# Mixture-of-experts stage: split fp32r products in groups of 256 columns replaced by plain fp32 products in groups of 512 columns, read straight from the load rings

## The reference

```python
logits = (xt @ w_router).astype(jnp.float32)
top_v, top_e = lax.top_k(logits, TOP_K)          # 2 of 8 experts
gates = jax.nn.softmax(top_v, -1)
...
def expert_block(args):
    tok, e = args
    xb = x_pad[tok]                              # up to 128 tokens of expert e
    return (jax.nn.silu(xb @ wg[e]) * (xb @ wu[e])) @ wd[e]
...
y = jnp.zeros((n + 1, D_MODEL), jnp.float32).at[buf_tok].add(yb... * buf_gate[:, None])
```

## Time and profile before

| | us |
|---|---|
| median of three runs | 2461.19 |
| the profiled execution, its own time | 2464.63 |
| its span, first to last instruction | 2462.8 |
| TensorE matmul busy / weight load busy | 2159.2 / 1740.0 |
| VectorE / ScalarE / GpSimd busy | 1315.7 / 1067.0 / 143.0 |
| first expert product to last added result | 1607.2 to 2448.4 |

### The profile page before, as it was taken

One profiled execution on the slowest core, in us unless ns is written; L12 is line 12 of the kernel. 1 busy time (PEld: TensorE's weight loads), 2 busy tenths in 40 slices (PEclk: granted clock), 3 DMA queues, 4 the chain that ended last, 5 costly groups with the idle time before them and its releaser, 6 DMA issues. The chain is left out here.

```text
span 2462.8 us, 38086 instructions
## 1 busy us (share of the span) xinstructions
PE 2159.2 (88%) x15542; PEld 1740.0 (71%) x15543; DVE 1315.7 (53%) x1913; ACT 1067.0 (43%) x1688; POOL 143.0 (6%) x176
## 2 busy tenths in 40 slices
PE   6986997799976898888878887699999999999997
PEld 4765996699954675577644454588778787787876
DVE  4125233444313465326733231488888888788885
ACT  3112321333213455224442330267666766667664
POOL 5001140000003100100000000000000000000000
PEclk8997998899988888856889998799999999999998
DMA  5100002554285542203024323489999999999993
GB/s 196 69 1 18 20 21 91 171 165 154 76 254 218 201 158 68 33 1 137 1 111 171 155 110 69 144 288 355 337 319 321 335 329 338 329 324 332 326 338 114
DMA packets 309634, 443.24 MB, mean 180 GB/s; under 512 B 60855, under 2 KB 273031, under 8 KB 306256
## 3 DMA queue, kind: packets, MB, share of 16 engines
q1 hardware_dynamic: 305706, 373.53, 46.1%
q0 software_dynamic: 3456, 67.11, 6.7%
q10 hardware_dynamic: 294, 0.11, 0.0%
HBM read 435.35 MB, written 13.67 MB: 182 GB/s over the span
## 5 line engine op out<-in xcount | busy, mean ns | idle before, releaser
L2763 DVE TENSOR_TENSOR moe.w_gate_up_lo<-mw.w_gate_up,moe.w_gate_up_hi 128x2048 fp32r<-128x2048 f32 x176 | 402.6, 2291 | 121.5 <-ACT moe.w_gate_up_hi L2696 121.3
L2696 ACT CAST moe.w_gate_up_hi<-mw.w_gate_up 128x2048 fp32r<-128x2048 f32 x176 | 335.7, 1909 | 161.5 <-PE moe.b L1050 161.5
L1048 PE MATMUL moe.b<-moe.w_gate_up_hi,moe.x_block_hi 128*128 128x512 f32 x704 | 277.3, 394 | 0.0
L1050 PE MATMUL moe.b<-moe.w_gate_up_hi,moe.x_block_lo 128*128 128x512 f32 x704 | 275.5, 391 | 0.0
L1049 PE MATMUL moe.b<-moe.w_gate_up_lo,moe.x_block_hi 128*128 128x512 f32 x704 | 275.1, 391 | 0.0
L2702 ACT CAST moe.w_down_hi<-mw.w_down 128x1024 fp32r<-128x1024 f32 x176 | 185.2, 1052 | 94.6 <-PE moe.b L1050 79.1
L2763 DVE TENSOR_TENSOR moe.w_down_lo<-mw.w_down,moe.w_down_hi 128x1024 fp32r<-128x1024 f32 x176 | 208.1, 1218 | 18.0 <-ACT moe.w_down_hi L2702 18.0
L1048 PE MATMUL moe.b<-moe.w_down_hi,moe.hidden_t_hi 128*128 128x512 f32 x352 | 148.6, 422 | 21.2 <-issue 18.8
L1050 PEld LDWEIGHTS moe.b<-moe.w_gate_up_hi,moe.x_block_lo 128*128 128x128 f32 x704 | 132.7, 188 | 28.5
L1048 PEld LDWEIGHTS moe.b<-moe.w_gate_up_hi,moe.x_block_hi 128*128 128x128 f32 x704 | 133.1, 189 | 26.3
L1049 PEld LDWEIGHTS moe.b<-moe.w_gate_up_lo,moe.x_block_hi 128*128 128x128 f32 x704 | 133.0, 189 | 26.2
(11 more groups left out here) (615 smaller groups left out, 4187.0 us busy)
## 6 DMA issues: line engine op xcount, KB each, us to landing
mw.w_gate_up<-in_moe_w_gate SPq DMA_DIRECT2D x176, 512.0 KB, 5.9
mw.w_gate_up<-in_moe_w_up SPq DMA_DIRECT2D x176, 512.0 KB, 7.2
mw.w_down<-in_moe_w_down SPq DMA_DIRECT2D x176, 512.0 KB, 6.0
rin.w_rkv<-in_rw_w_rkv SPq DMA_DIRECT2D x3, 4096.0 KB, 18.2
ffn.w<-in_ffn_w_gate SPq DMA_DIRECT2D x11, 1024.0 KB, 5.4
ffn.w<-in_ffn_w_up SPq DMA_DIRECT2D x11, 1024.0 KB, 8.0
ffn.w<-in_ffn_w_down SPq DMA_DIRECT2D x10, 1024.0 KB, 6.0
out_win_kv_sample<-in_state_win_kv SPq DMA_DIRECT2D x1, 8128.0 KB
```

What stands on the lines that cost most here:

```text
L1048: nc.tensor.matmul(out, w_hi, x_hi, start=start, stop=False)
L1050: return nc.tensor.matmul(out, w_lo, x_hi, start=False, stop=stop)
L2696: nc.scalar.copy(gu_hi[:, j % HR], M.wgu[:, j % M.RGU]).then_inc(gu_high, 1)
L2763: return nc.vector.tensor_tensor(out, x, high, ALU.subtract)
```

## The change

In `stage_moe` the split is gone. The normed rows are one fp32 tensor `M.x`, the products are single plain fp32 matmuls whose moving operand is the loaded piece itself, the groups are 512 columns wide (5 of 512 and one of 256 for each expert), gate and up have a bank each, and one buffer each of `H`, `silu`, `hidden_t` and `y` is left. A load piece has two (for the group of 256: four) of the eight row blocks, the rings have 12 pieces of 8 KB and 8 of 4 KB for each partition, and SP refills when TensorE has used a piece. The order on TensorE is `gate_up(T)`, `down(T - 1)`, `turn(T)`. `ahead` fills the larger rings. In `stage_moe_rest` only the gather is changed alike. The diff, cut to its core:

```diff
@@ stage_route, ahead and the block after it
-                for out, src in gate_up_half(M, io, j):
+                for out, src in gate_up_piece(M, io, j):
...
-                    nc.scalar.copy(M.xh[0:m, t, 512 * (n % 2):512 * (n % 2) + 512], bank[2 + n][0:m, :]).then_inc(ev, 1)
+                    nc.scalar.copy(M.x[0:m, t, 512 * (n % 2):512 * (n % 2) + 512], bank[2 + n][0:m, :]).then_inc(ev, 1)
...
-                    nc.vector.tensor_tensor(M.xl[0:m, t, c], bank[2 + n][0:m, :], M.xh[0:m, t, c], ALU.subtract)
...
-                step(nc.vector.tensor_copy(M.gate2[:, :, :, 0], M.gate[:, :, :]))
-                step(nc.vector.tensor_tensor(M.gate2[:, :, :, 1], M.gate[:, :, :], M.gate2[:, :, :, 0], ALU.subtract))
@@ loads
+SG = -(-F_FF // 512)
+PIECES_E = 4 * (SG - 1) + 2
+def piece(r):
+    return (r // 4, 512, 2 * (r % 4), 2) if r < 4 * (SG - 1) else (SG - 1, 256, 4 * (r - 4 * (SG - 1)), 4)
+def gate_up_piece(M, io, j):
+    e, r = divmod(j, PIECES_E)
+    g, w, k, n = piece(r)
+    out = M.wgu[:, j % M.RGU].rearrange("p (k n) -> p k n", n=2 * w)
     for i, name in enumerate(("moe_w_gate", "moe_w_up")):
+        yield out[:, :, w * i:w * i + w], io[name][0, e, P * k:P * k + P * n, 512 * g:512 * g + w].rearrange("(k p) n -> p k n", p=P)
@@ stage_moe, SP
+                for T in range(NGT):
+                    for j in pieces(T):
+                        if j >= M.RGU:
+                            sp.wait_ge(gu_used, j - M.RGU + 1)
+                            for out, src in gate_up_piece(M, io, j):
+                                sp.dma_start(out, src).then_inc(M.gu_in[j % M.RGU], 16)
+                    for T2 in ([T - 2] if T < NGT - 1 else range(T - 2, NGT)):
+                        for u in range(first_row(T2), first_row(T2) + tiles(T2)) if T2 >= 0 else ():
+                            if u >= M.RD:
+                                sp.wait_ge(d_used, u - M.RD + 1)
...
@@ stage_moe, TensorE
+                def gate_up(T):
+                    n, w = T // SG, width(T)
+                    if T:
+                        pe.wait_ge(hid, T)
...
+                    for j in pieces(T):
+                        _, _, k0, nk = piece(j % PIECES_E)
+                        pe.wait_ge(M.gu_in[j % M.RGU], 32 * (j // M.RGU + 1))
+                        weights = M.wgu[:, j % M.RGU].rearrange("p (k n) -> p k n", n=2 * w)
+                        for k in range(k0, k0 + nk):
+                            for i in range(2):
+                                last = nc.tensor.matmul(bank[i][:, 0:w], xe[:, n % 2, k, :], weights[:, k - k0, w * i:w * i + w],
+                                                        start=(k == 0), stop=(k == DC - 1))
                         last.then_inc(gu_used, 1)
...
+                def down(T):
+                    n, g = divmod(T, SG)
+                    pe.wait_ge(ht, T + 1)
                     if g == 0 and n:
+                        pe.wait_ge(y_a, n)
+                        pe.wait_ge(y_v, n)
+                    for q in range(tiles(T)):
+                        u = first_row(T) + q
+                        pe.wait_ge(M.d_in[u % M.RD], 16 * (u // M.RD + 1))
                         for half in range(2):
+                            last = nc.tensor.matmul(bank[4 + half][:, :], HT[:, q, :], M.wd[:, u % M.RD, 512 * half:512 * half + 512],
+                                                    start=(g == 0 and q == 0), stop=(g == SG - 1 and q == tiles(T) - 1))
                         last.then_inc(d_used, 1)
...
+                for T in range(NGT + 1):
+                    n, i = divmod(T, SG)
+                    if T < NGT:
+                        gate_up(T)
+                    if T:
+                        down(T - 1)
+                    if T < NGT:
+                        turn(T)
+                    if n and n < NE and i == 1:
...
+                        scatter(n - 1, range(4))
+                    if n and n < NE and i == 2:
+                        scatter(n - 1, range(4, DC))
+                    if n + 1 < NE and i == 3:
+                        gather(n + 1)
+                    if n + 1 < NE and i == 4:
+                        turn_sel(n + 1)
+                scatter(NE - 1, range(DC))
@@ build
-                M.RGU, M.RD = 6, 3
-                M.wgu, M.wd = mw.sb("w_gate_up", [P, M.RGU, 4, 2 * GW]), mw.sb("w_down", [P, M.RD, D])
+                M.RGU, M.RD = 12, 8
+                M.wgu, M.wd = mw.sb("w_gate_up", [P, M.RGU, 4 * 512]), mw.sb("w_down", [P, M.RD, D])
```

More of the change, by code:

```diff
@@ L2553, in stage_moe @@
[L2553 to L2575, removed]
+        NGT = NE * SG
+        xe = s.sb("x_block", [P, 2, DC, P])
@@ L2576, in stage_moe, with scatter_bank @@
+        def scatter_bank(n, c):
+            return bank[(3, 6, 7)[c % 3]] if n + 1 < NE else bank[(0, 1, 2, 3, 6, 7)[c % 6]]
         with nc.Block() as block:
@@ L2578, in _ @@
             def _(sp):
[L2579 to L2595, removed]
+                for T in range(NGT):
[8 more added lines that the diff above has]
+                                sp.wait_ge(d_used, u - M.RD + 1)
+                                out, src = down_rows(M, io, u)
+                                sp.dma_start(out, src).then_inc(M.d_in[u % M.RD], 16)
@@ L2613, in gather @@
                     last.then_inc(gathered, 1)
                 def turn_sel(n):
[L2617 to L2621, removed]
-                        last = nc.tensor.matmul(bank[7][:, 0:2], sel[:, t, :], M.gate2[:, n, t, :], start=(t == 0), stop=(t == 2))
@@ L2639, in turn @@
[L2639 to L2644 removed]
+                    pe.wait_ge(xe_a, n + 1)
+                    pe.wait_ge(xe_v, n + 1)
+                    for t in range(3):
+                        nc.tensor.transpose(bank[6][:, P * t:P * t + P], sel[:, t, :], G.ident[:, :])
@@ L2672, in _, with scatter @@
-                for r in range(2):
-                    gather(0, r)
-                turn_sel(0)
-                for t in range(STEPS):
-                    if t < NGT:
-                        gate_up(t)
-                    if 1 <= t <= NGT:
-                        turn(t - 1)
-                    if 2 <= t <= NGT + 1:
-                        down(t - 2)
-                    if scatter_at(t) is not None:
-                        scatter(scatter_at(t), (t - SCATTER) % NG)
-                    for r in range(2):
-                        if next_at(t, GATHER + r):
-                            gather(next_at(t, GATHER + r), r)
-                    if next_at(t, TURN):
-                        turn_sel(next_at(t, TURN))
+                def scatter(n, chunks):
+                    pe.wait_ge(y_a, n + 1)
+                    pe.wait_ge(y_v, n + 1)
+                    pe.wait_ge(selt_ready, n + 1)
+                    for c in chunks:
+                        banks = 3 if n + 1 < NE else 6
+                        if c >= banks:
+                            pe.wait_ge(added, DC * n + c - banks + 1)
+                        nc.tensor.matmul(scatter_bank(n, c)[:, 0:NT], y[:, P * c:P * c + P], selt[:, n % 2, :],
+                                         start=True, stop=True).then_inc(spread, 1)
@@ L2736, in _ @@
[L2736 to L2758 removed]
+                x_block(0)
@@ L2835, in stage_moe_rest @@
+                add(NE - 1, range(DC))
 def stage_moe_rest(nc, G, M, io):
```

286 lines of the change are left out of this document (98 added, 188 removed).

## The result

The changed kernel takes **2635.26 us** (median of four runs, 2630.34 to 2641.46) and the kernel before, in runs beside it on the same chip, 2459.5 us (four runs): a ratio of **1.0716, 95% interval 1.0684 to 1.0747**.

What follows compares the result with a forecast made beforehand. The prediction took TensorE to set the pace of the expert stage, with loads keeping up. Its terms, 169 + 13 - 2 = +180 us on the profiled 2464.6, gave 2645 us, range 2620 to 2682.

Steps and rivals of the forecast that it cites:

- The price of a product: Expert products of 512 columns: one plain fp32 product costs 0.860 us in place of 0.680, 908 us for eight experts.
- Weight loads not fully hidden: Rival: each of 2112 expert-product records pays 11.5 ns more for its weight load, adding 24 us, 2669 us; chance 0.05.
- The rest of the stretch: TensorE's other work between first expert product and last add; with the products 1010 us, before 841, so +169 us.
- the first group's bare chain: Expert stage's first group: silu and gated product stand uncovered between its products and its transposes, about 3 us.
- the 2 us for the lower clock: First expert products run at 1.2 GHz until the clock rises, 2 us lost, as before.
- The stall that goes: Change of experts: TensorE's 2.69 us stall goes because a `gate_up` of 13.8 us covers the copy of y.
- Single buffers: Rival: silu, gated product and handovers in the expert stage not covered by `down`, 77 us lost, 2722 us; chance 0.03.
- waits that could come: Expert stage loads: 275 GB/s asked for against 333 moved now, so costed at nothing; the bound if below 258 GB/s.
- The loads ahead: Norm's block: it can't end before SP has issued 32 loads in place of 15, +13 us; bounds +2 and +26.
- The block after it: From the router to the first expert product: fewer gate steps and no copies between the gather's halves, -2 us.
- Faster: Rival: expert-product records cost 0.2265 us as in fp32r, loads at 333 GB/s become the bound, 2430 us; chance 0.03.

Runs made afterwards that it cites:

- experiment 2: The changed kernel with half of the products of `down` left out, all loads and waits kept; 2489.72 us.
- experiment 4: The kernel before, with the result rows `y` split ahead of the weights of the same step; 2434.78 us, ratio 0.9877.
- experiment 3: The changed kernel with half of the gate, up and `down` products left out, all loads kept; 2287.62 us.
- experiment 5: The kernel before with only the `down` products in plain fp32, gate and up still split into fp32r; 2518.47 us, ratio 1.0216.

## Why the prediction was right, point by point

The mechanism held: TensorE sets the pace, and the price of a product makes the loss. That the total came so close is in part luck. The stretch, the block after it and the rest came out 8 us below the forecast; the loads ahead (1 us above) and work that the change doesn't touch (4 us) made up for more than half of it.

**The price of a product.** Right. 0.430 us a record was taken from two stages that have nothing to do with experts; the changed kernel has 0.429, and experiment 2 gives 0.858 for a whole product. The rival *Weight loads not fully hidden* falls with it. The rule of the Trainium skill's page "TensorE: Matmul & The Clock Gate", section "Back-to-back issue gap", that I set against the rows, 131 ns for each matmul, fits none of these streams (0.2265 us for fp32r, 0.429 for half a plain product).

**The rest of the stretch.** 1005.8 us for 1010. Records at 0.429 take 1.4 us off, the first group's bare chain was 1.7 us (1633.43, 32 records behind 1619.69, to 1635.14) for 3, and the 2 us for the lower clock did not come: the first 32 records run at full speed from the first.

**The stall that goes.** It is gone, as put, and it was absent from the sum already, so no term rests on its size. I read it as 2.69 us; with the slow records behind it it cost 4.3 at six of the seven changes (experiment 4). For a change that only removes it the gain is 30 us, not 19.

**Single buffers, and waits that could come.** Rightly put at nothing: TensorE was busy for 100 of 100 us. The handovers lie beside `down`.

**The loads ahead.** +13.9 for +13, by the right mechanism and two sizes that were off. SP is held by runs: in the changed kernel the tenth load of 256 runs is the first to take over 1 us (1564.58), behind 2,304 runs or 4.7 MB, and in experiment 4 the sixth of 512 runs, behind 2,560 runs or 2.6 MB; by bytes the two would be alike. But a held load takes 1.27 us, not 1.42, since 2 KB runs move 408 GB/s where 1 KB runs moved 348. (The 1.42 was too low for the kernel before as well: it is the issue alone, and from 1560.60 to 1569.72 its starts are 1.52 us apart.) And the eight pieces of `down`, which I let go free, took 0.76 us each. That the two errors cancel is luck.

**The block after it.** The mis-sized term: -5.1 us for -2. The gather has no wait between its halves and its 48 records are one dense row of 8.2 us; from its first row to the first product are 10.0 us for 14.4. The wait that went was 1.25 us. The larger part I had not thought of: in that row the granted clock already rises, from 0.50 to 1.00 at about 1615, and a record of the gather then starts some 0.12 us behind the last instead of 0.21. This is also why the first products ran at full speed.

**The rival *Faster*.** Its condition failed, since a product costs 0.858 us. Its time was wrong too: I let the loads go on at 333 GB/s, the rate of the kernel before with its runs of 1 KB. Experiment 3 puts the limit for the changed kernel's longer runs at 410 GB/s, so that what I gave as 2430 us would have been near 2290, an estimate from experiment 3's 2287.62.

## What to carry to other kernels

Count records and their distance before splitting or unsplitting a product: here a plain fp32 product is two records of 0.43 us, three fp32r ones are 0.68 us, and freeing VectorE and ScalarE of some 630 and 510 us changes nothing while TensorE sets the pace. A DMA share of 0.99 is not yet a limit in GB/s: with longer runs the same engines moved 410 instead of 333; take products away and look what the rate becomes. Loads issued ahead cost time when a block has to wait for the queue that issues them: put them where that queue has nobody waiting.

## What the runs showed of the hardware

- Runs of 2 KB went at 408 GB/s and runs of 1 KB at 348, both with the DMA engines full (1.05 and 1.09); over the whole expert stage of experiment 3 the changed kernel's runs (2 and 4 KB, 1 KB in the last groups) gave 409 to 411.
- A wait that the profile files under "issue" was a wait for another engine's work: the 18.8 us went when the rows of `y` were split earlier.
- Behind a stall of 2.7 us TensorE ran at a granted clock of 0.50 for some 3.5 us at six of seven places in the kernel before and at four of seven in experiment 5, and at 1.00 throughout at the others; what decides it is open.
